# Gate and up of three feed-forwards as seven products of quarter size in a transformer trunk on one core

## The chip, the cores and the metric

The kernel runs on one core of one Trainium2 chip, as one launch. The metric is the device time of that launch in microseconds (us), the median of three runs. The times of single instructions come from one profiled execution. The engines are named as the profile names them: PE is TensorE (matmuls) and PEld its weight loads, DVE is VectorE, ACT is ScalarE, POOL is GpSimd, SP is SyncE, which here only issues DMAs.

## What is computed

A decoder trunk of two layers over 512 tokens of width 1024, in float32. Each layer is a feed-forward, a mixer and a second feed-forward, all added to the residual `h`:

```
h = h + 0.5 * swiglu(rmsnorm(h, ffn1_norm[l]), ffn1_w_gate_up[l], ffn1_w_down[l])
u = rmsnorm(h, mix_norm[l])            # layer 0: gated DeltaNet, layer 1: forgetting attention
h = h + concatenate([main, mem_out]) @ w_out[l]
h = h + 0.5 * swiglu(rmsnorm(h, ffn2_norm[l]), ffn2_w_gate_up[l], ffn2_w_down[l])

def swiglu(x, w_gate_up, w_down):      # w_gate_up: 1024 x 5632, w_down: 2816 x 1024
    gate, up = jnp.split(x @ w_gate_up, 2, axis=-1)
    return (jax.nn.silu(gate) * up) @ w_down
```

After layer 0 one projection of the normed residual gives the keys, values and gates that layer 1 attends to. The trunk ends with an rmsnorm.

## The kernel before

**Layout.** `h` lies transposed in SBUF, as 8 tiles of 128 columns of the model by 512 tokens. A float32 product is made of three passes in the fp32r type: each operand is split into a rounded part and a rest (`x_hi`, `x_lo`; `w_hi`, `w_lo`), and hi*hi, hi*lo and lo*hi are summed in PSUM (`split_products`, lines 628 to 632).

**Phases.** In order: up0, down0, gdnin0 (projections and DeltaNet), wout0, up1, down1, kv0, up2, down2, foxin0 (projections and attention), wout1, up3, down3, final. `up` is the gate and up half of a feed-forward, `down` its second half. The change touches up1, up2 and up3, the phases ahead of them (wout0, kv0, wout1) and behind them (down1 to down3). up0 stays.

**A unit of an up phase.** An up phase is 22 units. A unit makes 128 columns of gate and the same 128 columns of up for 512 tokens: 8 slices of the model's 1024 columns, times 2 outputs, times 3 passes, which is 48 matmuls of 128x512 (`unit`, line 648). Two units alternate in everything: in `raw`, `w_hi` and `w_lo` (slot u % 2) and in two pairs of PSUM banks. For each unit
- SP loads 1 MB of weights to `raw` in two DMAs as soon as the rest of the unit two before is cut (`load_gate_up`, line 486, waits for `lo_ready`),
- ACT rounds them to `w_hi` (`round_hi`, line 1359) and DVE subtracts to `w_lo` (`cut_lo`, line 1887),
- after the unit's last matmul (`unit_done`) DVE moves gate and up from PSUM to `gate_up` times `rstd`, the rmsnorm's factor per token (`scaled`, line 1910), ACT takes the silu (line 1521), POOL multiplies (line 2657), ACT rounds the product to `hid_hi` (line 1525) and DVE cuts `hid_lo` (line 2066).

Each engine runs its own instructions in the order written. They meet through semaphores only.

**Around an up phase.** The last matmuls of wout or kv complete `h` two tiles at a time. DVE adds them to `h` (line 2457), ACT rounds the tile times its gain to `x_hi` (`feed_hi`) and DVE cuts `x_lo` (`feed_lo`). ACT squares each tile and POOL adds the squares up (`add_square`, line 2624). In wout phases PE sums them over partitions behind the first up unit (`spread_sum`), ACT takes the root, and DVE the reciprocal, `rstd` (line 1907). A tile of a down phase is 22 slices of `hid` by 3 passes, 66 matmuls. Before the first of them PE waits for half of `hid` at a time.

Of the kernel before, what the change touches and what calls it, by code (L numbers as in the profile page):

```python
# [118 lines left out]
def build_trunk(nc, mem, x, ffn1_norm, ffn1_gu, ffn1_down, mix_norm, ffn2_norm, ffn2_gu, ffn2_down,  # L119
# [22 lines left out]
    with ExitStack() as ctx:  # L142
# [73 lines left out]
        x_diag = place("x_diag", [P, SEQ], at=pair_at + 6144)  # L216
        late = HEAD_UNITS * SEQ * 4
# [27 lines left out]
        mpt_at = mixer.next  # L245
# [81 lines left out]
        y_rms = y_cols.put("y_rms", [P, TT])  # L327

# [38 lines left out]
        def over_heads(a, n=HEADS):  # L367
# [28 lines left out]
        hid_hi_ready, hid_ready = sem("hid_hi_ready"), sem("hid_ready")  # L396

# [50 lines left out]
        kv_spilled, c_spilled = [sem(f"kv_spilled{b}") for b in range(2)], sem("c_spilled")  # L448
        v_back, k_back, c_back = sem("v_back"), sem("k_back"), sem("c_back")
# [169 lines left out]
        def _(pe):  # L619
# [120 lines left out]
            for name in phases:  # L740
# [87 lines left out]
                elif kind == "up":  # L828
                    unit(u, g, x_hi, x_lo, feed=KT * feeds_before[fed_by[name]])
                    if fed_by[name] != "kv0":  # L830
                        spread_sum(fed_by[name])
                    unit(u + 1, g + 1, x_hi, x_lo)
                    with pe.Fori(0, NP // 2 - 1) as i:
                        for j in range(2):
                            unit(u + 2 + j, g + 2 + j, x_hi, x_lo, i)
                elif name == LAST_DOWN:
                    free = bank_of(g)

                    def turn_residual(c):

                        if c >= TT:
                            pe.wait_ge(y_moved, c - TT + 1)
                        for t in range(TT):
                            last = nc.tensor.transpose(ps[:, TT + c % TT, t * P:(t + 1) * P],
                                                       h[:, c, t * P:(t + 1) * P], ident[:])
                        last.then_inc(y_turned, 1)

                    for x in range(2):
                        for n, tiles in enumerate(LAST_TILES):
# [24 lines left out]
                            last.then_inc(unit_done, 1)  # L874
                            if x == 0 and 1 <= n <= KT // 2:
# [8 lines left out]
                elif kind == "gdnin":  # L884
# [13 lines left out]
                    def gram_product():  # L898
# [9 lines left out]
                        last.then_inc(gram, 1)  # L908
# [1880 lines left out]
```

## Time and profile before

| | us |
|---|---|
| median of 3 runs | 1965.64 |
| lowest and highest run | 1965.41, 1966.4 |
| span of the profiled execution | 1963.3 |
| up1, up2, up3 in that span | 240.3, 239.4, 240.3 |
| busy: PE, PEld, DVE, ACT, POOL | 1955.6, 1609.9, 895.2, 742.0, 379.3 |

The span is the time from the first to the last instruction of the profiled execution, and the result behind it differs from it by the launch (2.3 us here). A busy PE says only that matmuls were in flight: they overlap, each being recorded with its latency, so PE's pace is read from the distance between their starts. A group of instructions has the mean time of one. "Idle before" names what an engine waited for. The up phases are 720 us of the span.

### The profile page before, as it was taken

Reading aid. Unit: us, or ns where it says so; the run is one execution under the profiler, and the core shown is the slowest. Engines: PE = TensorE matmul, PEld = TensorE weight load, DVE = VectorE, ACT = ScalarE, POOL = GpSimd, SP = SyncE. Lnnn points to the kernel's source line nnn. Section 1 sums busy time; section 2 is a strip of 40 time slices with the busy share of each in tenths; the row PEclk is TensorE's granted clock in tenths of the full one; section 3 lists DMA queues with packets and bytes.
Section 4 is the critical chain, followed back from the end, with each engine's and each line's share of the span. In section 5 each row is a group of like instructions: output and inputs, shape, how many; then the busy total and the mean of one; then the engine's idle time right before and its main releaser. Section 6 shows DMA issues by size and latency. Waiting matters only on the chain.

```text
span 1963.3 us, 24695 instructions
## 1 busy us (share of the span) xinstructions
PE 1955.6 (100%) x9733; PEld 1609.9 (82%) x9733; DVE 895.2 (46%) x891; ACT 742.0 (38%) x908; POOL 379.3 (19%) x265
## 2 busy tenths in 40 slices
PE   9999999999999999999999999999999999999998
PEld 8888888888877888888888888888887788888887
DVE  6544334378866533433334433433346553333223
ACT  5422222245545444432222443432235453434213
POOL 1312221112813321211010121211011032121100
PEclk9999999999999999999999999999999999999999
DMA  6343323344221333332334433333351133332321
GB/s 195 95 122 105 107 74 88 106 138 131 87 56 44 103 94 103 91 94 87 90 98 153 126 90 103 92 87 89 101 198 44 43 107 103 90 104 78 118 97 65
DMA packets 313971, 196.16 MB, mean 100 GB/s; under 512 B 18543, under 2 KB 304896, under 8 KB 313394
## 3 DMA queue, kind: packets, MB, share of 16 engines
q1 hardware_dynamic: 309872, 182.29, 32.2%
q10 hardware_dynamic: 3138, 9.79, 1.5%
q0 software_dynamic: 896, 3.16, 0.4%
q8 instruction: 47, 0.77, 0.2%
q14 instruction: 18, 0.15, 0.0%
HBM read 188.75 MB, written 6.46 MB: 99 GB/s over the span
## 4 chain that ended last, share of the span: by engine, by line
PE 97%; DVE 2%; ACT 1%; issue 0%; DMA 0%; DVEq 0%; ACTq 0%
PE ps L630 30%; PE ps L632 30%; PE ps L631 30%; PE ps L1301 1%; PE ps L1275 1%; PE ps L713 0%; PE ps L1286 0%; PE ps L735 0%; PE ps L725 0%; PE ps L1128 0%; PE ps L1006 0%; PE ps L1122 0%; PE ps L985 0%; PE ps L1102 0%; PE ps L936 0%
## 5 line engine op out<-in xcount | busy, mean ns | idle before, releaser
L630 PE MATMUL ps<-x_hi,w_hi 128*128 128x512 f32 x1790 | 706.5, 395 | 0.3
L632 PE MATMUL ps<-x_hi,w_lo 128*128 128x512 f32 x1790 | 697.1, 389 | 0.0
L631 PE MATMUL ps<-x_lo,w_hi 128*128 128x512 f32 x1790 | 696.9, 389 | 0.0
L1366 ACT ACTIVATE w_hi<-raw 128x2048 fp32r<-128x2048 f32 (+2 forms) x180 | 315.8, 1754 | 726.7 <-PE ps L632 726.7
L1892 DVE TENSOR_TENSOR w_lo<-raw,w_hi 128x2048 fp32r<-128x2048 f32 (+1 forms) x179 | 394.7, 2205 | 244.1 <-ACT w_hi L1366 244.1
L630 PEld LDWEIGHTS ps<-x_hi,w_hi 128*128 128x128 f32 x1790 | 336.2, 188 | 75.1 <-issue 4.1
L632 PEld LDWEIGHTS ps<-x_hi,w_lo 128*128 128x128 f32 x1790 | 336.0, 188 | 70.3
L631 PEld LDWEIGHTS ps<-x_lo,w_hi 128*128 128x128 f32 x1790 | 336.3, 188 | 68.1 <-issue 1.0
L1914 DVE TENSOR_TENSOR gate_up<-ps,rstd 128x1024 f32<-128x1024 f32 x88 | 107.8, 1225 | 326.7 <-PE ps L632 326.2
L2657 POOL TENSOR_TENSOR gate_up<-gate_up 128x512 f32<-128x512 f32 x66 | 145.8, 2210 | 565.8 <-ACT gate_up L1521 565.8
L630 PE MATMUL ps<-hid_hi,w_hi 128*128 128x512 f32 x528 | 205.4, 389 | 0.0
L631 PE MATMUL ps<-hid_lo,w_hi 128*128 128x512 f32 x528 | 205.4, 389 | 0.0
L632 PE MATMUL ps<-hid_hi,w_lo 128*128 128x512 f32 x528 | 205.4, 389 | 0.0
L2624 POOL TENSOR_TENSOR square_sum<-square_sum,gate_up 128x512 f32<-128x512 f32 x40 | 69.3, 1732 | 412.5 <-ACT gate_up L1381 350.3
L630 PEld LDWEIGHTS ps<-hid_hi,w_hi 128*128 128x128 f32 x528 | 99.1, 188 | 20.7
L631 PEld LDWEIGHTS ps<-hid_lo,w_hi 128*128 128x128 f32 x528 | 99.1, 188 | 20.6
L632 PEld LDWEIGHTS ps<-hid_hi,w_lo 128*128 128x128 f32 x528 | 99.1, 188 | 20.4
L2066 DVE TENSOR_TENSOR hid_lo<-gate_up,hid_hi 128x512 f32 (+1 forms) x66 | 45.7, 693 | 136.0 <-ACT hid_hi L1525 136.0
L1525 ACT ACTIVATE hid_hi<-gate_up 128x512 f32 (+1 forms) x66 | 41.9, 634 | 159.2 <-POOL gate_up L2657 159.2
L630 PE MATMUL ps<-w_hi,hid_hi 128*128 128x512 f32 x176 | 68.8, 391 | 0.0
L632 PE MATMUL ps<-w_hi,hid_lo 128*128 128x512 f32 x176 | 68.5, 389 | 0.0
L631 PE MATMUL ps<-w_lo,hid_hi 128*128 128x512 f32 x176 | 68.5, 389 | 0.0
(334 smaller groups left out, 1645.3 us busy)
## 6 DMA issues: line engine op xcount, KB each, us to landing
raw<-in_ffn_w_gate_up SPq DMA_DIRECT2D x174, 512.0 KB, 5.0
raw<-in_ffn_w_down SPq DMA_DIRECT2D x48, 384.0 KB, 3.7
raw<-in_ffn_w_down SPq DMA_DIRECT2D x48, 320.0 KB, 3.1
raw<-in_gdn_w_in SPq DMA_DIRECT2D x26, 512.0 KB, 4.8
raw<-in_ffn_w_down SPq DMA_DIRECT2D x20, 512.0 KB, 4.3
raw<-in_w_out SPq DMA_DIRECT2D x16, 512.0 KB, 4.4
raw<-in_kv_w SPq DMA_DIRECT2D x12, 512.0 KB, 4.8
raw<-in_mem_w_kv SPq DMA_DIRECT2D x8, 512.0 KB, 4.2
```

What stands on the lines that cost most here:

```text
L630: nc.tensor.matmul(dst, hi, xh, start=first, stop=False)
L631: nc.tensor.matmul(dst, hi, xl, start=False, stop=False)
L632: return nc.tensor.matmul(dst, lo, xh, start=False, stop=last)
L1275: nc.tensor.matmul(ps[:, 4 + n % 2, 0:(i + 1) * P], fq[:, hd, i * P:(i + 1) * P], fk[:, hd, 0:(i + 1) * P], start=True, stop=True).then_in ...
L1301: last = nc.tensor.matmul(ps[:, b1 + hd % 2, i * P:(i + 1) * P], fv[:, s, hd * P:(hd + 1) * P], fpt[m % 2][:, s * P:(s + 1) * P], start=s ...
L1366: nc.scalar.activation(w_hi[s][:, 0:n], raw[s][:, 0:n], ACT.Copy).then_inc(hi_ready, 1)
L1525: nc.scalar.activation(hid_hi[:, bass.ds(at, 1), :], gate_up[:, j, 0:1, :], ACT.Copy).then_inc(hid_hi_ready, 1)
L1892: nc.vector.tensor_tensor(w_lo[s][:, 0:n], raw[s][:, 0:n], w_hi[s][:, 0:n].bitcast(F32), ALU.subtract).then_inc(lo_ready, 1)
L1914: nc.vector.tensor_tensor(dst, src, by, ALU.mult).then_inc(evac, 1)
L2066: nc.vector.tensor_tensor(hid_lo[:, bass.ds(at, 1), :], gate_up[:, j, 0:1, :], hid_hi[:, bass.ds(at, 1), :].bitcast(F32), ALU.subtract).th ...
L2624: nc.gpsimd.tensor_tensor(square_sum[:, 0:tokens], square_sum[:, 0:tokens], gate_up[:, b, 0, 0:tokens], ALU.add).then_inc(sum_ready, 1)
L2657: nc.gpsimd.tensor_tensor(gate_up[:, j, 0, :], gate_up[:, j, 0, :], gate_up[:, j, 1, :], ALU.mult).then_inc(prod_ready, 1)
```

## The change

**The scheme.** In up1 to up3 the product of a unit is seen as a 2x2 block product: the model's tiles are taken as even and odd ones (4 pairs), the outputs as gate and up, the tokens as two halves of 256. Seven products of blocks replace the eight: each is 4 pairs by 3 passes, 12 matmuls of 128x256, so 84 in a unit. Three products take a weight block as loaded (`direct`, 1536 words of a row), four take a sum of blocks (`sums`, four blocks of 512 words, S1 to S4). Four take plain quarters of `x` or its difference T1, and three the differences T4, T2, T3 of `x` (`t_x`).

**Sums of weights.** POOL makes S1 and S3 (`first_sum`, `third_sum`), DVE S2 and S4 (`second_sum`). ACT rounds and DVE cuts the direct blocks (1536 words), S1 with S2, and S4 with S3 (1024 each). Direct parts now always lie in the one slot of `w_hi` and `w_lo`, sums in the other, so each is rewritten while its own unit runs, once the products that read it are done.

**Results.** DVE puts gate and up together from seven parts in PSUM with four additions and scales gate alone; ACT first copies the first product's part (`first_taken`). POOL writes the product of silu(gate) and up to a new `hid`. Up is no longer scaled: the down phases scale by `rstd` instead (one more DVE instruction for each of 8 tiles in down1 and down2; `y_half` in down3). The split of `hid` into `hid_hi` and `hid_lo` moves behind the units: 22 tiles in a row from the last unit on, since its place holds `t_x` and `sums` until then, and down waits for them tile by tile.

**Feeding.** wout0, kv0 and wout1 also make the differences of `x` (`even_source`, `pair_columns`) and the first unit's sums (`seven_lead`, `seven_lead_more`, `seven_lead_last`). Many semaphores are shared under new names with the same meaning (`left`).

```diff
+            def seven_unit(name, u, g, n, i=0, spread=False):
...
+                pe.wait_ge(direct_lo, NP * x + n + 1 + 2 * i)
+                bank_free(g + n, i)
+                seven_product(to[1], direct_at(u, 0), operands("B11")).then_inc(product_done, 1)
+                seven_product(to[4], direct_at(u, 1), operands("T4"))
+                seven_product(to[2], direct_at(u, 2), operands("B21")).then_inc(product_done, 1)
+                pe.wait_ge(sums_lo, (NP + 1) * x + n + 2 + 2 * i)
+                seven_product(to[5], sum_at(u, S1), operands("T1")).then_inc(product_done, 1)
+                seven_product(to[6], sum_at(u, S2), operands("T2")).then_inc(product_done, 1)
+                pe.wait_ge(lo_ready, u + n + 1 + 2 * i)
+                pe.wait_ge(part_taken, NP * x + n + 1 + 2 * i)
+                seven_product(to[3], sum_at(u, S4), operands("B22")).then_inc(product_done, 1)
+                if spread:
+                    pe.wait_ge(rms_ready, sums_before[fed_by[name]] + 1)
+                seven_product(to[7], sum_at(u, S3), operands("T3")).then_inc(unit_done, 1)
...
-                    if hid_wait is not None:
-                        pe.wait_ge(hid_ready, hid_wait + (half + 1) * HALF)
+                        if hid_wait is not None:
+                            pe.wait_ge(hid_ready, hid_wait + n + 1)
...
+                    def step(n, j, i=0, more=True, root=False):
...
+                            last_sums(n, i)
+                            if root:
+                                root_mean_square(fed_by[name], rstd[:], bank=bank_of(g + 1) + 5)
+                            silu(n - 1, 1 - j, i)
+                        take_first(n, j, i)
+                        if more:
+                            act.wait_ge(product_done, at + 2 + 2 * DONE * i)
...
+                            nc.scalar.activation(direct(w_hi, slot(u)), direct_blocks(slot(u + n + 1))[:, :, 1:4, :],
+                                                 ACT.Copy).then_inc(direct_hi, 1)
...
+                        if more:
+                            first_sums(n + 1, at + 4, i)
...
+                        even_source(name, n)
+                        odd_hi(name, n)
...
+                        if n == 2:
+                            seven_lead(feeds[name], u + 4)
+                        even_hi(name, n)
+                        t_hi(name, n)
...
+                    def partial_sums(n, j, i=0):
...
+                        nc.vector.tensor_tensor(two_halves(up), over_heads(first_taken[:, j, :], 2),
+                                                two_halves(ps[:, b + 1, :]), ALU.add).then_inc(gate_step, 1)
+                        dve.wait_ge(gate_step, 4 * (NP * x + n) + 1 + 8 * i)
+                        nc.vector.tensor_tensor(two_halves(gate), over_heads(up[:, TOK:], 2),
+                                                two_halves(ps[:, b + 4, :]), ALU.add).then_inc(gate_step, 1)
...
                     def step(n, j, i=0):
...
+                        if n:
+                            gates(n - 1, 1 - j, i)
+                            if n == 1 and normed:
+                                last_sums(n)
+                                reciprocal_of_rms(fed_by[name], rstd[:])
+                            gate_scale(n - 1, 1 - j, i)
+                            if n > 1 or not normed:
+                                last_sums(n, i)
+                        second_sum(name, u, n + 1, i)
+                        direct_cut(name, u, n + 1, i)
...
+                        partial_sums(n, j, i)
+                        first_sums(n + 1, i)
+                        up_second(n, j, i)
...
+                        first_sum(u, n + 1, sums_used + n + 2, i)
+                        if n:
+                            product(n - 1, 1 - j, i)
+                        third_sum(u, n + 1, i)
```

**The order on DVE in the loop over units.** One unit of up1's loop before; the names are the kernel's tiles.

```order
L1914 TENSOR_TENSOR gate_up<-ps,rstd 128x1024 [waits unit_done]
L1891 REGISTER_ALU
L1892 TENSOR_TENSOR w_lo_64<-raw_62,w_hi_63 128x2048 [waits hi_ready]
L2064 REGISTER_ALU
L2066 ISA [waits hid_hi_ready]
L2066 TENSOR_TENSOR hid_lo<-gate_up,hid_hi 128x512
```

The same engine and loop after the change, without its register rows:

```order
L2498 TENSOR_TENSOR gate_up<-gate_up,ps 128x512 [waits gate_step]
...
L2504 TENSOR_TENSOR gate_up<-gate_up,rstd 128x512 [waits evac]
...
L2304 TENSOR_TENSOR w_lo_67<-sums,w_hi_66 128x1024 [waits hi_ready]
...
L2289 TENSOR_TENSOR sums<-sums,raw_62 128x512 [waits pool_sum]
L2292 TENSOR_TENSOR sums<-raw_62,sums 128x512 [waits dve_sum]
L2298 TENSOR_TENSOR w_lo_64<-raw_62,w_hi_63 128x1536 [waits direct_hi]
...
L2480 TENSOR_TENSOR gate_up<-first_taken,ps 128x512 [waits prod_ready]
...
L2483 TENSOR_TENSOR gate_up<-gate_up,ps 128x512 [waits gate_step]
...
L2304 TENSOR_TENSOR w_lo_67<-sums,w_hi_66 128x1024 [waits sums_hi]
...
L2490 TENSOR_TENSOR gate_up<-gate_up,ps 128x256 [waits gate_step]
```

Three instructions of a unit became ten; four of the ten read PSUM, six read SBUF alone.

**The order on POOL in the same loop.** Before, one unit:

```order
L2657 TENSOR_TENSOR gate_up<-gate_up 128x512 [waits silu_ready]
```

After, one unit:

```order
L3168 TENSOR_TENSOR sums<-raw_62 128x512 [waits sums_lo]
L3207 REGISTER_ALU
L3208 ISA [waits silu_ready]
L3208 TENSOR_TENSOR hid<-gate_up 128x512
L3175 REGISTER_ALU
L3176 TENSOR_TENSOR sums<-raw_62 128x512 [waits lo_ready]
```

The product now stands between two sums of weights.

**The order on DVE from the last wout0 tiles into up1.** After the change only, from the sums of unit 0 on; before, the same stretch is one addition to `h`, two cuts of `x_lo`, one of weights and the reciprocal.

```order
L2289 TENSOR_TENSOR sums<-sums,raw_62 128x512 [waits pool_sum]
L2292 TENSOR_TENSOR sums<-raw_62,sums 128x512 [waits dve_sum]
L2298 TENSOR_TENSOR w_lo_64<-raw_62,w_hi_63 128x1536 [waits direct_hi]
L2304 TENSOR_TENSOR w_lo_64<-sums,w_hi_63 128x512 [waits sums_hi]
L2304 TENSOR_TENSOR w_lo_67<-sums,w_hi_66 128x1024 [waits sums_hi]
...
L2270 TENSOR_TENSOR t_x<-t_f,t_x 128x3x256 [waits t_hi_ready]
L2304 TENSOR_TENSOR w_lo_67<-sums,w_hi_66 128x512 [waits hi_ready]
L2289 TENSOR_TENSOR sums<-sums,raw_65 128x512 [waits pool_sum]
L2292 TENSOR_TENSOR sums<-raw_65,sums 128x512 [waits dve_sum]
L2298 TENSOR_TENSOR w_lo_64<-raw_65,w_hi_63 128x1536 [waits direct_hi]
```

All of it is queued ahead of what PE waits for: L2298 first for unit 0, last for unit 1.

## Rows read from the trace of the kernel before

**Rows 1.** The page: busy time of the engines, and what the chain of waits lies on.

```profile
PE 1955.6 (100%) x9733; PEld 1609.9 (82%) x9733; DVE 895.2 (46%) x891; ACT 742.0 (38%) x908; POOL 379.3 (19%) x265
...
PE 97%; DVE 2%; ACT 1%; issue 0%; DMA 0%; DVEq 0%; ACTq 0%
```

**Rows 2.** Windows over up1 and up2: length, PE, PEld, DVE, ACT, POOL, clock, DMA.

```profile
663.20:903.50 240.30, 240.30 (x1059) 198.65 (x1059) 95.94 (x68) 95.66 (x89) 50.86 (x23) 1.00 0.34 93
1095.00:1334.40 239.40, 239.40 (x1058) 198.23 (x1057) 92.17 (x67) 93.32 (x85) 46.08 (x22) 1.00 0.34 95
```

**Rows 3.** Timeline of PE (start, length): matmuls of 512 columns, then of 256.

```profile
88.20 0.39 PE L631 MATMUL ps<-x_lo,w_hi 128*128 128x512 f32 x1
...
90.46 0.39 PE L632 MATMUL ps<-x_hi,w_lo 128*128 128x512 f32 x1
...
91.04 0.28 PE L630 MATMUL ps<-xm_hi,w_hi 128*128 128x256 f32 x1
...
95.84 0.28 PE L631 MATMUL ps<-xm_lo,w_hi 128*128 128x256 f32 x1
```

**Rows 4.** Timeline of DVE in up1 (start, length, idle before).

```profile
707.86 1.23 DVE L1914 TENSOR_TENSOR gate_up<-ps,rstd 128x1024 f32<-128x1024 f32 x1 [3.87 <-PE ps L632]
709.82 2.29 DVE L1892 TENSOR_TENSOR w_lo<-raw,w_hi 128x2048 fp32r<-128x2048 f32 x1 [0.73 <-ACT w_hi L1366]
```

**Rows 5.** Groups of DVE and ACT by form (count, busy, mean ns, idle before).

```profile
L2214 DVE TENSOR_TENSOR low<-low,decay 128x1536 f32<-128x1536 f32 x1 | 1.8, 1759 | 0.2 <-ACT decay L1699 0.2
L1892 DVE TENSOR_TENSOR w_lo<-raw,w_hi 128x1024 fp32r<-128x1024 f32 x4 | 4.9, 1225 | 17.5 <-ACT w_hi L1366 17.5
L2232 DVE TENSOR_TENSOR z<-ps,rstd 128x512 f32<-128x512 f32 x6 | 4.1, 686 | 1.7 <-PE ps L632 1.6
L2364 DVE TENSOR_TENSOR v_new<-v_tok,ps 128x256 f32<-128x256 f32 x7 | 2.9, 421 | 3.5 <-PE ps L1102 3.5
L1907 DVE RECIPROCAL rstd<-rstd 128x512 f32<-128x512 f32 x5 | 16.8, 3354 | 19.5 <-ACT rstd L1385 19.5
L1366 ACT ACTIVATE w_hi<-raw 128x1024 fp32r<-128x1024 f32 x4 | 4.2, 1060 | 23.9 <-PE ps L632 23.9
L1699 ACT ACTIVATE decay<-decay 128x1536 f32<-128x1536 f32 x1 | 1.5, 1492 | 1.4 <-DVE decay L2204 1.4
L1525 ACT ACTIVATE hid_hi<-gate_up 128x512 f32 x60 | 38.1, 634 | 145.0 <-POOL gate_up L2657 145.0
```

**Rows 6.** Timeline of POOL in up1.

```profile
875.01 1.45 POOL L2657 TENSOR_TENSOR gate_up<-gate_up 128x512 f32<-128x512 f32 x1 [9.43 <-ACT gate_up L1521]
884.46 2.88 POOL L2657 TENSOR_TENSOR gate_up<-gate_up 128x512 f32<-128x512 f32 x1 [8.00 <-ACT gate_up L1521]
```

**Rows 7.** Timeline of DVE beside the second of them, and beside POOL in down0.

```profile
883.89 2.29 DVE L1892 TENSOR_TENSOR w_lo<-raw,w_hi 128x2048 fp32r<-128x2048 f32 x1 [0.73 <-ACT w_hi L1366]
...
295.26 0.75 DVE L1898 SCALAR_TENSOR_TENSOR x_lo<-h,gains,x_hi  x1 [1.37 <-ACT x_hi L1369]
295.93 2.72 DVE L1892 TENSOR_TENSOR w_lo<-raw,w_hi 128x1408 fp32r<-128x1408 f32 x1
...
295.75 1.41 POOL L2624 TENSOR_TENSOR square_sum<-square_sum,gate_up 128x512 f32<-128x512 f32 x1 [12.92 <-ACT gate_up L1381]
```

**Rows 8.** Timeline of DVE and POOL in the DeltaNet: a DVE read of PSUM first.

```profile
575.45 1.23 DVE L2223 COPY k<-ps 128x1024 f32<-128x1024 f32 x1 [2.52 <-PE ps L1006]
...
576.79 1.69 DVE L1936 TENSOR_TENSOR mp<-mp,m_stat 128x1024 f32<-128x1024 f32 x1
...
575.50 1.90 POOL L2723 TENSOR_TENSOR k_tok<-k_tok,gate_exp 128x1024 f32<-128x1024 f32 x1 [38.07 <-PE ps L1006]
```

**Rows 9.** Groups of POOL by form, flat rows and short ones.

```profile
L2647 POOL TENSOR_TENSOR mem_sum<-mem_sum,mem_sq 128x256 f32<-128x256 f32 x7 | 5.2, 736 | 8.7 <-ACT mem_sq L1499 8.3
L2702 POOL TENSOR_TENSOR tri<-tri,tri_tmp 96x256 f32<-96x256 f32 x1 | 1.1, 1061 | 0.1
```

**Rows 10.** The page's DMA issues: the weights of gate and up, with the time to landing.

```profile
raw<-in_ffn_w_gate_up SPq DMA_DIRECT2D x174, 512.0 KB, 5.0
```

More of the change, by code:

```diff
@@ L75 @@
 MEM_SCORES_BESIDE = 12
+SEVEN = ("up1", "up2", "up3")
+TOK = SEQ // 2
+PAIRS = KT // 2
+BLOCK_W = PAIRS * P
+DIRECT_W = 3 * BLOCK_W
+T4, T2, T3 = 0, 1, 2
+S1, S2, S4, S3 = 0, 1, 2, 3
+DONE = 5
+T4_TILES, T2_TILES, T3_TILES, SUM_TILES, TAKEN_TILES = 2, 6, 10, 14, 18
 def fox_block(n):
@@ L216, in build_trunk @@
         x_diag = place("x_diag", [P, SEQ], at=pair_at + 6144)
+        TILE_B = SEQ * 4
+        t_x = place("t_x", [P, 3, 2, PAIRS, TOK], F32R, at=lo_at + T4_TILES * TILE_B)
+        t_f = place("t_f", [P, 3, 2, PAIRS, TOK], at=lo_at + T4_TILES * TILE_B)
+        sums = place("sums", [P, 4, BLOCK_W], at=lo_at + SUM_TILES * TILE_B)
+        taken = Region(lo_at + TAKEN_TILES * TILE_B, (NP - TAKEN_TILES) * TILE_B)
+        first_taken = taken.put("first_taken", [P, 2, TOK])
+        even_f = {name: place(f"even_f_{name}", [P, PAIRS, SEQ], at=h_at + at)
+                  for name, at in (("wout0", 12 << 10), ("kv0", 12 << 10), ("wout1", 40 << 10))}
         late = HEAD_UNITS * SEQ * 4
@@ new lines, in seven_part, with direct_at, sum_at @@
+            def seven_part(dst, weights, x_of, kk, first=False, last=False):
+                w_s, at = weights(kk)
+                xh, xl = x_of(kk)
+                return split_products(dst, w_hi[w_s][:, at:at + P], w_lo[w_s][:, at:at + P], xh, xl,
+                                      first and kk == 0, last and kk == PAIRS - 1)
+            def direct_at(u, q):
+                return lambda kk: (slot(u), (3 * kk + q) * P)
+            def sum_at(u, r):
+                return lambda kk: (slot(u + 1), r * BLOCK_W + kk * P)
@@ new lines, in seven_regions, with seven_product @@
+            def seven_regions(g0):
+                b = bank_of(g0)
+                lo_cols, hi_cols = slice(0, TOK), slice(TOK, SEQ)
+                return {1: ps[:, b, lo_cols], 3: ps[:, b, hi_cols],
+                        2: ps[:, b + 1, lo_cols], 6: ps[:, b + 1, hi_cols],
+                        4: ps[:, b + 4, lo_cols], 5: ps[:, b + 4, hi_cols], 7: ps[:, b + 5, lo_cols]}
+            def seven_product(dst, weights, x_of):
+                for kk in range(PAIRS):
+                    last = seven_part(dst, weights, x_of, kk, first=True, last=True)
+                return last
@@ new lines, in _ @@
+                    step(0, 0)
+                    step(1, 1, root=fed_by[name] != "kv0")
+                    with act.Fori(0, NP // 2 - 2) as i:
+                        for j in range(2):
+                            step(2 + j, j, i)
+                    step(NP - 2, 0)
+                    step(NP - 1, 1, more=False)
+                    for tile in range(4, T3_TILES):
+                        split_hi(tile)
+                    silu(NP - 1, 1)
+                    round_hi(u + NP + 1)
+                    for tile in range(T3_TILES, NP):
+                        split_hi(tile)
@@ L1828, in _ @@
-                            act.wait_ge(f_a, 2)
-                            nc.scalar.activation(t, t, ACT.Ln, bias=ones[0:HEADS, 0:1]).then_inc(f_a, 1)
-                        if n == HEADS - 1:
-                            for c in range(KT - 1):
-                                act.wait_ge(x_free, N_REL * releases[name] + c + 1)
-                                feed_hi(x_hi[:, c, :], h[:, c, :], gains[:, gain + c:gain + c + 1])
+                            act.wait_ge(row_d, left["row_d"] + 1)
@@ L2075, in _ @@
+                    split_lo(3)
+                    partial_sums(NP - 1, 1)
+                    up_second(NP - 1, 1)
+                    split_lo(4)
+                    gates(NP - 1, 1)
+                    gate_scale(NP - 1, 1)
+                    for tile in range(5, T3_TILES):
+                        split_lo(tile)
+                    cut_lo(u + NP + 1)
+                    for tile in range(T3_TILES, NP):
+                        split_lo(tile)
                 elif name == LAST_DOWN:
```

632 lines of the change are left out of this document (493 added, 139 removed).

## The prediction

> **What bounds the kernel now.** Read first the page's engine line and its chain of waits [rows 1]: PE is busy all through, and the chain lies on it for 97%. Then the windows over up1 and up2 [rows 2]: PE fills both at a granted clock of 1.00 (2.4 GHz), while DVE is busy for 96 and 92 of 240 us, ACT for 96 and 93, POOL for 51 and 46. Up3 reads like up1. The profiled execution (1963.3 us, and 2.3 outside) equals the median to 0.1 us, so its rows can be added to 1965.6. 239.4 us for 22 units is 10.88 us a unit, and up1's and up3's further 0.5 us is `spread_sum`. The weights' loads take 5.0 us to land, half a unit [rows 10]: SP isn't the question. So a shorter product counts in full, until another engine needs more than PE. A busy share of 40% leaves room, but the change fills just that.
>
> **PE, removed and added.** Ten starts of 512-column matmuls take 2.26 us and forty of 256 columns 4.80 us [rows 3]: 226 and 120 ns each; by the length of the phase, 239.4 / (22 x 48), the first is 226.7, which I take. A unit goes from 48 x 0.2268 = 10.89 us (the phase gives the same) to 84 x 0.120 = 10.08. Seven eighths would be 9.53: half the width costs more than half the time. The gain is 0.81 us a unit, 53 us over 66 units, if PE stays the bound. The Trainium skill, "TensorE: Matmul & The Clock Gate", section Back-to-back issue gap, gives columns / 2.4 GHz + 2.5 ns for a lone matmul; by that, an estimate, a unit goes from 10.36 to 9.17 and gains 1.19. The rows contradict it in both widths (226.8 and 120 ns against 215.8 and 109.2), and I go by the rows.
>
> **DVE, a steady unit.** Before: 1.23 to empty PSUM, 2.29 for the cut [rows 4], 0.69 for `hid_lo`, 4.2 us. After: six operations of 512 (gate's second part, its scale, S2, S4, two partial sums) at 0.69, two cuts of 1024 at 1.22, one of 1536 at 1.76, one addition of 256 at 0.42 [rows 5]. That is 4.14 + 2.44 + 1.76 + 0.42 = 8.76. An instruction in a row starts 0.08 us before the one ahead is through (295.93 behind 295.26 + 0.75 [rows 7]), one that needs the other's result just behind it; with five or so such overlaps I take 8.40. Alone it would fit under 10.08, with 1.7 us to spare.
>
> **DVE against POOL.** POOL used to have one operation of 512 a unit, now three. Alone that takes 1.45 us, beside a cut 2.88 [rows 6]: it started 0.57 us into the cut and ended 1.16 us after its end at 886.18 [rows 6, 7]. Nor is DVE spared: a cut of 1408 took 2.72 us behind a POOL addition that had begun 0.18 us before [rows 7], where 1.22 for 1024 and 1.76 for 1536 [rows 5] put it at some 1.62; and `mp` took 1.69 instead of 1.23 until POOL's multiplication was through [rows 8]. Reading PSUM, a DVE copy kept its 1.23 beside POOL [rows 8]. So operations of SBUF inputs alone exclude each other between DVE and POOL, first come first served, and PSUM reads are free. Of POOL's 1.45 us the first 0.3 need no lock and some 1.15 do: that is what it worked on after the cut's end. The Trainium skill, "SBUF — State Buffer", section Who interferes with whom, says the same and against this change: the port pair that the two share is an exclusive lock held for the whole instruction, taken by a DVE instruction with two SBUF inputs. By the page all 1.45 would count, 4.35 for three; the rows show 1.15 each.
>
> Now lay the two orders beside each other. `first_sum` is released by the first sums' cut and runs beside `up_second` and the gate's addition, both PSUM reads: only its last 0.31 us holds up the scale. `product` is released by the silu (512 words, about the 0.63 of `hid_hi` [rows 5]) and two handoffs of under 0.1, some 0.75 us behind the scale, while DVE is in the last sums' cut (1.22), so it is next in line and has the lock just ahead of S2: 1.09. `third_sum` is released by that same cut and starts behind `product`, while S2 runs; it gets the lock ahead of S4: 0.98. Sum 2.38, and DVE's unit is 8.40 + 2.38 = **10.78 us, 0.70 over PE's 10.08**. DVE becomes the bound: the direct cut of the next unit, last in this row, is what PE waits for (`direct_lo`). Of 0.81 us a unit 0.11 is left. POOL (3 x 1.45, with its waits 5.3) and ACT (1.06 + 0.63 for the silu + at most 0.63 for the copy + 1.49 + 1.06 = 4.9 us [rows 5]) have room; what ACT costs hangs on its place in the chain.
>
> **Start of up1 and up3.** Here DVE has the new feeding (four differences and three cuts where two cuts stood), and POOL its additions of squares. Laid out from the end of the last but two weights of wout, with the same durations: the last wout unit waits 0.84 us for its weights' cut, which stands behind the second pair's feeding; unit 0 of up waits 2.15 for the direct cut, behind S2 and S4, each held up 1 us by an addition of squares; inside unit 0, the last pair's `x` and T parts come 2.85 late. Unit 1 waits 3.8 for its direct cut: `first_sum` stands behind the last addition of squares (1.45), then come first_sum 1.45, S2 0.69 + 1.13, S4 0.69 and the cut 1.76. In unit 1 PE's P3 waits 2.6 for `first_taken`: ACT's copy stands behind the silu, that behind the scale, that behind the reciprocal of 3.35 us [rows 5]. Unit 2 waits another 0.3. Sum 12.6, less two shorter units (1.6): **+11.0 us**. Before, the reciprocal was hidden: nobody but the evacuation two units on waited for it.
>
> **The phases.** Up1: +11.0; 19 units at 10.78 for 10.89, -2.0; the last at PE's pace, -0.8; and down1. Its first tile, 66 x 0.2268 = 15.0 us on PE, now waits tile by tile for 22 cuts of 0.69 (15.2) on DVE, which start about 3 us after the units' end (scale 0.69, silu 0.62, product 1.45 and one rounding 0.63); 18.6 in all, +3.6. Together +11.8. Up3: the same start; down3 uses each tile of `hid` for four times as many matmuls (2.7 us), which hides the cuts: +8.2. Up2 is fed from kv0, with the squares and the reciprocal done: PE's pace for the first four units and the last (-4.0), 17 at 10.78 (-1.9), the same 0.8 ahead of its first unit, and +3.6 in down2: -1.5. The scale in down1 and down2 lies beside 15 us of PE, except behind the last tile: +0.5 with what hangs on it. Sum 11.8 + 8.2 - 1.5 + 0.5 = +19.0: **1985 us**. Within this case the handoffs may be 0.05 us longer each (10.89 a unit, +8 over three phases) or the start's waits 2 to 5 us shorter each: 1973 to 1997.
>
> **Rivals.**
> *PE stays the bound (faster, the other side).* Place: the turn of DVE's loop where `product` and `third_sum` stand. Price: what is blocked must stay under 10.08 - 8.40 = 1.68 us a unit; 2.38 is my sum. It does if one of the two falls beside the partial sums, which read PSUM, for instance because the scale comes later and `product` meets `second_sum` when that is already under way; then one block of 1 us goes. POOL's own delay is harmless. Then up1 gives -1.6 (start +11.0, 20 units x -0.81, down +3.6), up3 -5.2 (no down), up2 -14.2 (22 units, down2), the scales +0.5: 1945. If in addition the starts overlap better (unit 1 needs no more than 1 us), 1933. For it: POOL has 4.8 us of slack, and which of two comes first hangs on 0.1 us. Against it: in the steady order both sums' places are fixed by the same cut.
> *POOL's sums are slower.* No row of before shows a POOL operation that picks blocks of a row. 736 ns for a flat 128x256 and 1061 for the same 256 cut in short pieces [rows 9] bound it at 1.45 and 2.1 for 512; the sums' pieces are whole blocks of 128 or more words, nearest to the flat form. At 1.6, a unit is 11.08 (each 0.15 counts twice) and the sum is +19 + 0.3 x 19 x 3 = +36: 2002.
> *POOL's sums cost 1.35.* 10.48 a unit: 19 x 3 x 0.3 = 17 us less: 1967, no change.
> *The clock.* Before, no window shows less than 1.00 [rows 2], since PE never paused. Now it pauses for up to 3.8 us twice. If its clock falls to 1.2 GHz there, one unit of 10 us may run at half speed: up to +10 for a start, in the upper part of my range.
> *The change does less than it says:* the matmuls' count is plain in the code; excluded.
>
> **How the numbers follow.** DVE-bound as laid out 0.44, 1985 (1973 to 1997, slower). Slower sums on POOL 0.20, 2002 (slower). Shorter ones 0.08, 1967 (same). PE-bound 0.28 (faster), of it 0.20 near 1945 and 0.08 near 1933. The range leaves out the last and the tail above 2008: 1940 to 2008. A measurement here tells 0.2%, 4 us, from no change, so faster than 1961.7 is 0.28, between 0.08, above 1969.6 is 0.64.
>
> **What the profile after would show.** PE's 256-column starts 120 ns apart (else the gain is wrong). DVE busy for about 10.7 of each 10.8 us in up1's middle, PE's idle before P1 put down to `w_lo` of the direct cut; with PE bound, DVE idle before its gate addition instead. S2 and S4 at 1.7 us each where I take them blocked, at 0.69 where not. POOL's sums at 1.45. PE's third and second waits of 2 to 4 us in the first two units of up1 and up3, none such in up2. Tiles of `hid` in down1 0.69 us apart. The prediction is wrong if S2 and S4 are short: then the whole steady term turns to -0.8 a unit.

## The result, and the profile after

The changed kernel takes 1988.8 us (median of four runs, 1988.13 to 1990.04) against 1965.53 for the kernel before: a ratio of 1.012, 95% interval 1.0105 to 1.0134. It is slower by 23 us, the forecast was slower by 19 (1985.0).

The profile's page of the changed kernel: busy time of the engines, and the chain of waits. Before [rows 1], DVE was busy for 895 us and the chain lay on PE for 97%.

```profile
PE 1930.9 (97%) x12113; PEld 1688.2 (85%) x12113; DVE 1387.8 (70%) x1499; ACT 802.2 (40%) x1076; POOL 524.5 (26%) x397
...
PE 73%; DVE 14%; issue 6%; POOL 3%; ACT 2%; DMA 1%; DVEq 0%; SPq 0%; ACTq 0%; POOLq 0%
```

Two windows of the same kernel (length, PE, PEld, DVE, ACT, POOL, granted clock, DMA share, GB/s), one over 17 units in the middle of up1 and one over the first half of its unit 1:

```profile
700.00:880.00 180.00, 175.37 (x1429) 172.01 (x1428) 177.66 (x171) 74.76 (x85) 75.40 (x52) 1.00 0.36 99
683.00:690.00 7.00, 6.50 (x42) 6.50 (x43) 6.86 (x8) 1.99 (x3) 1.28 (x1) 0.76 0.03 9
```

DVE is busy for 177.7 of 180 us where it was busy for 96 of 240 [rows 2]. What PE waited for, over the whole span (total, times, longest); the kernel before shows none of these lines in its up and down phases:

```profile
PE ps L680 <- DVE w_lo L2298: 25.4, 63, 2.8
PE ps L680 <- DVE w_lo L2208: 11.4, 4, 5.8
PE ps L680 <- DVE hid_lo L2520: 5.2, 6, 1.0
PE ps L680 <- DVE t_x L2270: 2.9, 2, 1.6
PE ps L680 <- ACT first_taken L1746: 2.1, 2, 1.0
```

L2298 is the direct cut, 63 waits in 66 units. Its row in the steady part, and three matmul rows that give the pitch of 256 columns (compare rows 3): 0.12 us from start to start, ten steps in 1.20.

```profile
707.24 0.38 PE L680 MATMUL ps<-x_hi,w_hi 128*128 128x256 f32 x1 [0.28 <-DVE w_lo L2298]
...
714.53 0.28 PE L680 MATMUL ps<-x_hi,w_hi 128*128 128x256 f32 x1
...
715.73 0.28 PE L681 MATMUL ps<-x_lo,w_hi 128*128 128x256 f32 x1
```

A wait of 0.28 us in its latency's shadow costs a unit 0.5 us. The units of up1 start 17.0, 13.1, then 10.60 us apart (19 times, the last of them 10.66), and the last one takes 10.17. The stretches of the two executions, each from the start of its first matmul to that of the next stretch's (the first begins a quarter into the last wout0 unit but one):

| stretch (us) | before | after | difference | forecast |
|---|---|---|---|---|
| wout0's last two units and up1 | 259.4 | 264.5 | +5.1 | +8.2 |
| down1 | 119.7 | 123.3 | +3.6 | +3.6 |
| kv0 and up2 | 311.2 | 306.2 | -5.0 | -5.1 |
| down2 | 119.7 | 123.3 | +3.6 | +3.6 |
| foxin0, wout1, up3 | 380.2 | 389.9 | +9.7 | +8.2 |
| down3 and the end | 129.1 | 135.4 | +6.3 | 0 |

With -0.3 ahead of wout0 this is the 23.1 us between the two spans. The forecast's 0.5 us for the scales of down1 and down2 together is in no row.

One unit of DVE's row in up1 (start, length; idle before is shown where there is any), and POOL's of the same unit; the rows of before are rows 4, 6 and 7.

```profile
800.76 1.75 DVE L2298 TENSOR_TENSOR w_lo<-raw,w_hi 128x1536 fp32r<-128x1536 f32 x1
802.43 0.68 DVE L2480 TENSOR_TENSOR gate_up<-first_taken,ps 128x512 f32<-128x512 f32 x1
803.14 0.69 DVE L2483 TENSOR_TENSOR gate_up<-gate_up,ps 128x512 f32<-128x512 f32 x1
803.75 1.22 DVE L2304 TENSOR_TENSOR w_lo<-sums,w_hi 128x1024 fp32r<-128x1024 f32 x1
804.88 0.41 DVE L2490 TENSOR_TENSOR gate_up<-gate_up,ps 128x256 f32<-128x256 f32 x1
805.33 0.69 DVE L2498 TENSOR_TENSOR gate_up<-gate_up,ps 128x512 f32<-128x512 f32 x1
806.05 0.84 DVE L2504 TENSOR_TENSOR gate_up<-gate_up,rstd 128x512 f32<-128x512 f32 x1
806.81 1.21 DVE L2304 TENSOR_TENSOR w_lo<-sums,w_hi 128x1024 fp32r<-128x1024 f32 x1
807.94 1.78 DVE L2289 TENSOR_TENSOR sums<-sums,raw 128x512 f32<-128x512 f32 x1
809.76 1.67 DVE L2292 TENSOR_TENSOR sums<-raw,sums 128x512 f32<-128x512 f32 x1
811.36 1.75 DVE L2298 TENSOR_TENSOR w_lo<-raw,w_hi 128x1536 fp32r<-128x1536 f32 x1
...
805.04 1.30 POOL L3168 TENSOR_TENSOR sums<-raw 128x512 f32<-128x512 f32 x1 [4.75 <-DVE w_lo L2304]
807.74 1.44 POOL L3208 TENSOR_TENSOR hid<-gate_up 128x512 f32 x1 [1.40 <-ACT gate_up L1752]
809.14 1.75 POOL L3176 TENSOR_TENSOR sums<-raw 128x512 f32<-128x512 f32 x1
```

The reader sees ten DVE operations from 800.76 to 811.36 with nothing between them, and among six of 512 words two that take 1.78 and 1.67 us instead of 0.69. S2 (L2289) is through 0.54 us after POOL's product ends at 809.18; S4 (L2292) 0.54 us after POOL's third sum ends at 810.89. The third sum itself takes 1.75 instead of 1.30 since it waits for S2. The scale (L2504) loses 0.15 to the first sum, and the two additions beside that sum, which read PSUM, nothing.

### The profile page after: what moved, and what is told of

It reads as the page before. It is cut to its first block, busy times and chain, and to the rows that moved or that the text cites. A ratio compares the mean times of both kernels' runs of the same rounds, so it can differ in the third digit from the quotient of the medians.

```text
span 1986.4 us, 31460 instructions
## 1 busy us (share of the span) xinstructions
PE 1930.9 (97%) x12113; PEld 1688.2 (85%) x12113; DVE 1387.8 (70%) x1499; ACT 802.2 (40%) x1076; POOL 524.5 (26%) x397
## 4 chain that ended last, share of the span: by engine, by line
PE 73%; DVE 14%; issue 6%; POOL 3%; ACT 2%; DMA 1%; DVEq 0%; SPq 0%; ACTq 0%; POOLq 0%
PE ps L680 23%; PE ps L682 22%; PE ps L681 22%; DVE w_lo L2298 6%; POOL tri L3265 2%; POOL tri_tmp L3263 1%; DVE hid_lo L2520 1%; DVE w_lo L2208 1%; DVE sums L2289 1%; PE ps L1442 1%; PE ps L1468 1%; DVE rstd L2223 1%; DVE w_lo L2304 0%; ACT w_hi L1533 0%; PE ps L1453 0%
## 5 line engine op out<-in xcount | busy, mean ns | idle before, releaser
L680 PE MATMUL ps<-x_hi,w_hi 128*128 128x256 f32 (+1 forms) x1790 | 601.7, 336 | 29.0 <-DVE w_lo L2298 25.4
L682 PE MATMUL ps<-x_hi,w_lo 128*128 128x256 f32 (+1 forms) x1790 | 586.4, 328 | 0.0
L681 PE MATMUL ps<-x_lo,w_hi 128*128 128x256 f32 (+1 forms) x1790 | 586.0, 327 | 0.0
L2208 DVE TENSOR_TENSOR w_lo<-raw,w_hi 128x2048 fp32r<-128x2048 f32 (+2 forms) x113 | 245.4, 2172 | 176.2 <-ACT w_hi L1533 176.2
L680 PE MATMUL ps<-t_x,w_hi 128*128 128x256 f32 x792 | 225.0, 284 | 2.9 <-DVE t_x L2270 2.9
L681 PE MATMUL ps<-t_x,w_hi 128*128 128x256 f32 x792 | 224.8, 284 | 0.0
L682 PE MATMUL ps<-t_x,w_lo 128*128 128x256 f32 x792 | 224.5, 283 | 0.0
L1601 ACT ACTIVATE w_hi<-sums 128x1024 fp32r<-128x1024 f32 (+1 forms) x135 | 140.2, 1040 | 182.2 <-PE ps L682 159.7
L2304 DVE TENSOR_TENSOR w_lo<-sums,w_hi 128x1024 fp32r<-128x1024 f32 (+1 forms) x135 | 161.2, 1195 | 0.0
L680 PEld LDWEIGHTS ps<-t_x,w_hi 128*128 128x128 f32 x792 | 153.0, 193 | 3.3 <-DVE t_x L2270 3.3
L681 PEld LDWEIGHTS ps<-t_x,w_hi 128*128 128x128 f32 x792 | 152.7, 193 | 0.0
L682 PEld LDWEIGHTS ps<-t_x,w_lo 128*128 128x128 f32 x792 | 152.7, 193 | 0.0
```

The source lines that it names most:

```text
L680: nc.tensor.matmul(dst, hi, xh, start=first, stop=False)
L681: nc.tensor.matmul(dst, hi, xl, start=False, stop=False)
L682: return nc.tensor.matmul(dst, lo, xh, start=False, stop=last)
L1601: nc.scalar.activation(w_hi[s][:, at:at + (r1 - r0) * BLOCK_W], sums[:, r0:r1, :].rearrange("p r n -> p (r n)"), ACT.Copy).then_inc(signal, 1)
L2208: nc.vector.tensor_tensor(w_lo[s][:, 0:n], raw[s][:, 0:n], w_hi[s][:, 0:n].bitcast(F32), ALU.subtract).then_inc(lo_ready, 1)
L2304: nc.vector.tensor_tensor(w_lo[s][:, cols], sums[:, r0:r1, :].rearrange("p r n -> p (r n)"), w_hi[s][:, cols].bitcast(F32), ALU.subtract). ...
```

## Experiments

Every experiment is an edit of the changed kernel. Times stand against its 1988.8 us, and the kernel before ran at 1965.2 to 1965.5 beside each of them.

### x1: POOL's third sum behind the direct cut

```
 def third_sum(u, n, i=0, cuts=None):
     if n:
         pool.wait_ge(lo_ready, u + n + 2 * i)
+    if cuts is not None:
+        pool.wait_ge(direct_lo, cuts + 2 * i)
...
-    third_sum(u, n + 1, i)
+    third_sum(u, n + 1, i, NP * seven_index(name) + n + 2)
```

> The changed kernel with one more wait: POOL's third_sum starts only when DVE's direct cut of the same unit is through, so that it falls beside DVE's two partial sums, which read PSUM, instead of beside S4. Theory (DVE is the bound because POOL's operations lock it out): S4 falls from 1.58 to 0.69 us, a unit from 10.60 to PE's 10.08, 57 units x -0.52 = -30 us, 1959 us (1955 to 1963). Rival 1 (what is blocked only moves, onto the first sums' cut behind the partial sums): S4 short, but that cut 0.5 to 1 us longer, a unit of 10.4 to 10.6, 1977 to 1989. Rival 2 (a unit's length hangs on DVE's own work and the handoffs, not on POOL): no change.

Measured: 1952.12 us (1951.06 to 1952.68), ratio to before 0.9931 (0.9914 to 0.9948). The units are 10.08 us apart. The same part of a unit, DVE then POOL, in up1:

```profile
802.77 0.69 DVE L2292 TENSOR_TENSOR sums<-raw,sums 128x512 f32<-128x512 f32 x1
803.76 1.76 DVE L2298 TENSOR_TENSOR w_lo<-raw,w_hi 128x1536 fp32r<-128x1536 f32 x1 [0.30 <-ACT w_hi L1796]
805.44 0.68 DVE L2480 TENSOR_TENSOR gate_up<-first_taken,ps 128x512 f32<-128x512 f32 x1
806.15 0.69 DVE L2483 TENSOR_TENSOR gate_up<-gate_up,ps 128x512 f32<-128x512 f32 x1
806.76 1.29 DVE L2304 TENSOR_TENSOR w_lo<-sums,w_hi 128x1024 fp32r<-128x1024 f32 x1
...
805.67 1.30 POOL L3178 TENSOR_TENSOR sums<-raw 128x512 f32<-128x512 f32 x1 [3.47 <-DVE w_lo L2298]
```

The same sum, begun 0.23 us into the first partial sum, costs DVE 0.07 us (on the cut at 806.76) instead of 1: two operations that read PSUM cover it. S2's block by the product stays (S2 takes 1.70 us in the mean). DVE now waits for ACT (0.30), and a unit is PE's 84 x 0.12 again. One more wait on POOL gives 36.7 us, more than the 30 expected: in the profiled executions the three up phases are 32.4 us shorter, and down1, down2 and down3 1.5, 1.5 and 1.8, since the cuts of `hid` start earlier. Rival 1 and 2 are out. This version beats the kernel before by 13 us.

### x2: POOL's sums made short

```
-    nc.gpsimd.tensor_tensor(by_pair(sums[:, S1, :]), blocks[:, :, 0, :], blocks[:, :, 2, :],
+    nc.gpsimd.tensor_tensor(by_pair(sums[:, S1, :])[:, :, 0:w], blocks[:, :, 0, 0:w], blocks[:, :, 2, 0:w],
...
-    nc.gpsimd.tensor_tensor(by_pair(sums[:, S3, :]), blocks[:, :, 1, :], blocks[:, :, 0, :],
+    nc.gpsimd.tensor_tensor(by_pair(sums[:, S3, :])[:, :, 0:w], blocks[:, :, 1, 0:w], blocks[:, :, 0, 0:w],
```

(w is 128 in unit 0 of a phase and 4 in the others.)

> The changed kernel with POOL's two sums of weights cut to 4 x 4 words of a row in all units behind the first of a phase, so most of S1 and S3 keeps old values; every semaphore and all of DVE's, ACT's and PE's work stay. Theory (lock): without two of POOL's three operations a unit of up takes PE's 10.08 us; S4 0.69 and S2 0.69 to 1.75, as product still meets it or not; with the starts 1950 to 1957 us in all. Rival (DVE's own chain or ACT's order sets 10.60): units stay at 10.5 to 10.6, 1980 to 1988.

Measured: 1948.3 us in a single run, units 10.08 us apart, S4 0.72 us in the mean of 66 and S2 still 1.70:

```profile
L2289 DVE TENSOR_TENSOR sums<-sums,raw 128x512 f32<-128x512 f32 x66 | 112.1, 1699 | 8.3 <-POOL sums L3170 8.3
L2292 DVE TENSOR_TENSOR sums<-raw,sums 128x512 f32<-128x512 f32 x66 | 47.7, 722 | 2.3
```

The kernel leaves most of S1 and S3 unwritten, so it shows the time alone. S4 lost what the third sum took, S2 kept what the product takes. With DVE's own work untouched the unit fell to PE's 10.08, so 10.60 was POOL's doing.

### x4: unit 1's first sum ahead of the last two squares

```
 for c in range(KT):            # POOL, wout
     add_square(name, c % 2, c)
...
+    if c == 5:
+        first_sum(u + KT // 2, 1, (NP + 1) * seven_index(feeds[name]) + 2)
```

> The changed kernel with the first sum of unit 1 of up1 and up3 moved on POOL ahead of the last two additions of squares of wout. Theory (unit 1 waits 3.6 us for its direct cut since first_sum stands behind those additions, and the pause lowers PE's clock for some 1.5 us more): the wait falls to under 1 us, the slow matmuls behind it go, 2 x (3 + 1.4) = -9 us, 1980 us. Rival (DVE's work is what unit 1 waits for; the additions, now beside S2 and S4, lock it out for as long): the wait falls by 1 to 2 us, 1984 to 1987.

Measured: 1985.39 us, 3.4 less. The waits of PE in the last wout0 unit and the first two units of up1, the changed kernel and then this one:

```profile
PE ps L680 <- DVE w_lo L2298: 4.8, 2, 2.8
PE ps L680 <- ACT first_taken L1746: 1.0, 1, 1.0
```

```profile
PE ps L680 <- DVE w_lo L2298: 2.9, 2, 1.9
PE ps L680 <- ACT first_taken L1746: 2.5, 1, 2.5
```

The wait ahead of unit 1 falls from 2.83 us (not the expectation's 3.6) to 0.98, and the one for `first_taken` in unit 1 grows from 1.05 to 2.53: four fifths of the 1.85 us are given back at the next wait. DVE's own rows say why, S2 of unit 1 in the changed kernel, then S2, S4 and the direct cut in this one:

```profile
679.30 1.75 DVE L2289 TENSOR_TENSOR sums<-sums,raw 128x512 f32<-128x512 f32 x1 [3.87 <-POOL sums L3168]
```

```profile
675.87 1.79 DVE L2289 TENSOR_TENSOR sums<-sums,raw 128x512 f32<-128x512 f32 x1
677.69 1.68 DVE L2292 TENSOR_TENSOR sums<-raw,sums 128x512 f32<-128x512 f32 x1
679.29 2.84 DVE L2298 TENSOR_TENSOR w_lo<-raw,w_hi 128x1536 fp32r<-128x1536 f32 x1
```

The 3.87 us in which DVE stood idle for POOL's sum are gone, but now S4 and the direct cut, 0.69 and 1.75 us in the changed kernel, stand beside squares and the third sum and take 2.1 us more. That is the rival. My theory that POOL's queue alone held unit 1 falls.

### x5: ACT's copy ahead of silu in unit 1

```
         silu(n - 1, 1 - j, i)   # now only for n > 1
     take_first(n, j, i)
+    if n == 1:
+        silu(0, 0)
```

> The changed kernel with ACT's copy of unit 1's first product put ahead of silu of unit 0, which stands behind the scale and that behind the reciprocal. Theory (PE's wait of 1.05 us for first_taken in up1 and 1.02 in up3 is that order): both waits go, -2.4 us with what follows each, 1986.4 us. Rival (DVE has the rest of that stretch full, so that unit 2 waits for its direct cut instead): unit 2 starts when it did, 1988 to 1989.

Measured: 1988.77 us (1987.43 to 1990.24), no change. The wait for `first_taken` is gone, and the direct cut has a third one in the same stretch:

```profile
PE ps L680 <- DVE w_lo L2301: 6.2, 3, 2.8
```

It was 4.8 in two, and is 6.2 in three. Unit 1 and unit 2 start when they did (17.0 and 13.15 us apart). The rival holds: the direct cut of unit 2 starts on DVE at 694.57 instead of 694.74, and PE meets it there.

### x8: squares made short

```
-    add_square(name, c % 2, c)
+    add_square(name, c % 2, c, tokens=SEQ if c < 4 else 8)
```

> The changed kernel with POOL's additions of squares of tiles 4 to 7 in wout0 and wout1 cut to 8 of 512 tokens, so the norm ahead of up1 and up3 is that of half the model for most tokens. Theory (POOL's squares lock DVE out in the feeding, and hold up first_sum of unit 1): S2 and S4 of unit 0 0.69 instead of 1.78 and 1.70 us, unit 0 starts 2 us earlier, and unit 1's wait of 3.6 us falls to 1 or less; with the clock's share 4 to 6 us for each of up1 and up3, 1977 to 1981 us. Rival (the new feeding itself, seven DVE operations for each pair, sets the start): under 2 us for each, 1985 to 1988.

Measured: 1981.7 us in a single run, 7 less. Unit 0 of up1 takes 14.9 instead of 17.0 us and unit 0 of up3 13.5; the wait ahead of unit 1 is under 0.7 us; and again there is one of 2.15 us for `first_taken` (1.05 before). Counted over the stretches of the table, up1 is done 3.7 us sooner and up3 3.1. So POOL's squares and their place account for 3 to 4 us of each start, less than I expected. The rest I put down to the new feeding on DVE; no run took that away.

### x6 and x9: down weights earlier, in all three phases and in the last alone

```
+    round_hi(u + NP + 1)      # ACT, ahead of the last silu
     silu(NP - 1, 1)
-    round_hi(u + NP + 1)
...
-    for tile in range(5, T3_TILES):    # DVE
-        split_lo(tile)
+    split_lo(5)
     cut_lo(u + NP + 1)
+    for tile in range(6, T3_TILES):
+        split_lo(tile)
```

> The changed kernel with the second block of down weights rounded ahead of the last silu (ACT) and cut ahead of all but one of the tiles of hid that stood before it (DVE), in all three up phases. Theory (in down3 PE waits 3.7 us for this cut and then runs slow for 2 us): -5.5 us, 1983 us, down1 and down2 as before. Rival (the tiles of hid, now later, are waited for in its place): the wait in down3 becomes one for hid_lo of 1 to 2 us, and down1 and down2 are 1 to 2 us longer each, 1986 to 1990.

> The edit of x6 in up3 alone. In x6 down3 fell from 129.3 to 125.3 us while down1 and down2 grew by 2.9 and 1.8, where PE now waited for tiles of hid. Theory (it helps only where a tile of hid lasts PE 2.7 us): -4 us, 1984.8. Rival (down3's gain belongs to a shift that the other two made): no change.

Measured: 1989.53 (1987.14 to 1989.57) with all three, 1984.48 (1984.24 to 1984.58) with the last alone. In the first, down3 is 4.0 us shorter, but down1 2.9 and down2 1.8 longer: there a tile of `hid` lasts PE 0.68 us, and PE waits for the tiles that the cut pushed back. The waits in down1 of the first kernel, and the one left in down3 of the second (3.65 us in the changed kernel):

```profile
PE ps L680 <- DVE hid_lo L2520: 3.2, 2, 2.2
```

```profile
PE ps L680 <- DVE w_lo L2211: 0.9, 1, 0.9
```

So the cut that is early in one phase is late in the other, and the edit pays where a tile of `hid` is used for 12 matmuls.

### x11: the weights of wout's last unit cut earlier

```
+    if n == 1:
+        cut_lo(u + 3)
     feed_pair(name, n)
-    if n == 1:
-        cut_lo(u + 3)
```

(ACT's rounding of the same weights likewise ahead of its part of the feeding.)

> The changed kernel with the weights of wout's last unit rounded and cut ahead of the feeding of the second pair of tiles, in wout0 and wout1. In wout1 PE waits 5.84 us for that cut, which the prediction had at 0.8. Theory (DVE has feeding, cuts and sums without a gap from there to unit 0's direct cut, so this pause of PE is not on the path): the pause shrinks to under 1 us and unit 0 of up3 starts when it did, within 1 us of 1609; 1987 to 1990. Rival (the wait costs what it shows): unit 0 of up3 starts 4 to 6 us earlier, 1983 to 1985.

Measured: 1988.06 us (1987.74 to 1988.37), within 1 us of the changed kernel. PE's waits from 1575 to 1640 us, the changed kernel and this one:

```profile
PE ps L680 <- DVE w_lo L2208: 5.8, 1, 5.8
PE ps L680 <- DVE w_lo L2298: 3.5, 2, 2.8
```

```profile
PE ps L680 <- DVE w_lo L2298: 10.3, 2, 7.4
```

The pause of 5.8 us is gone, and a pause of 7.4 stands ahead of unit 0 of up3, which starts at 1608.05 instead of 1609.22. Half a microsecond of that was gained before down2; from the start of foxin0 to the end of up3 the kernels differ by 0.7 us. That is what the longest wait in the profile cost.

### x7 and x10: together

> Four edits together: third_sum behind the direct cut (as in x1), first_sum of unit 1 ahead of the last two squares (as in x4), in unit 1 of each phase ACT's copy of the first product ahead of silu, and the second block of down weights earlier in up3 alone. Theory (each takes away a wait of its own): from 1952.1 a unit 1 shorter by 2.5 us and by what the slow clock behind a pause costs, 1.4, in up1 and up3 (-8), -4 in down3: 1940 us (1937 to 1944). Rival (the starts hang on DVE's sum of work, and what is saved at one wait is met at the next): only down3's 4 us and 1 to 2 in each start, 1945 to 1948.

Measured: 1945.22 us (1941.92 to 1946.88), ratio to before 0.9901 (0.9884 to 0.9917). That is in the rival's range: against x1 down3 gave 3.8 us, up1 2.1 and up3 2.8 (229.0 us each). Unit 2 now waits for its direct cut, 1.5 us in up1 and up3, behind the reciprocal (the next expectation says 1.66 and 1.69).

> x7 with one more edit: in step 1 of each phase DVE makes unit 2's S2, S4 and direct cut ahead of the reciprocal and the scale of unit 0, and ACT takes silu of unit 0 last in that step. Theory (in x7 unit 2 waits 1.66 and 1.69 us for its direct cut, which stands behind the reciprocal's 3.35 us): that wait goes and nothing follows, -3.3 us from x7, 1942 us (1938 to 1944). Rival (the reciprocal now holds up the partial sums and the cut of unit 2's first sums, which P5 of unit 2 waits for): the wait turns up at P5, 1944 to 1947.

```
     gates(n - 1, 1 - j, i)
-    if n == 1 and normed: last_sums(n); reciprocal_of_rms(...)
-    gate_scale(n - 1, 1 - j, i)
+    if n == 1: last_sums(n)
     second_sum(name, u, n + 1, i)
     direct_cut(name, u, n + 1, i)
+    if n == 1: reciprocal_of_rms(...); gate_scale(0, 0)
```

Measured: 1944.13 us (1943.14 to 1944.77), ratio to before 0.9893 (0.9876 to 0.9909): 1 us from the former, inside the spread of both. The 1.5 us wait went and three came in unit 2 and 3 of up1, for the cuts of sums (0.40 and 0.88) and the direct cut (1.03). The rival again. It has the lowest median of all versions, 21 us ahead of the kernel before; against x7 nothing is shown, whose runs go down to 1941.92.

## Why the prediction came out right

**The pitch of the matmuls** (120 ns, 10.08 us a unit) was as read: the products take 84 x 0.12. By the formula of the Trainium skill for a lone matmul ("TensorE: Matmul & The Clock Gate", section Back-to-back issue gap) a unit would take 9.17 us, an estimate. It does not hold here: x1's units, with PE as the bound, take 10.08.

**DVE as the bound through the lock** was right in kind and nearly in size. Forecast blocks 0.31, 1.09 and 0.98 us; shown 0.15 for the scale, 1.09 for S2 and 0.98 for S4 in the unit above (in the mean of 66 units 0.13, 1.06 and 0.89). The unit came out at 10.60, not 10.78: the term that was mis-sized is the block of the scale, 0.16 of the 0.18 us, because POOL's first sum takes 1.30 us and not the 1.45 of its product, which I took for it; in 57 units the 0.18 is 10 us. The third sum is as short when nothing holds it up (1.30 in x1), yet S4's block came out at the 0.98 forecast with 1.45. So "each 0.15 counts twice" was not borne out, and the rival with sums of 1.35 was wrong in its own sum too: by that rule its unit is 10.58 and not 10.48.

The Trainium skill, "SBUF — State Buffer", section Who interferes with whom, calls the port pair of DVE and GpSimd an exclusive lock, which a DVE instruction with two SBUF inputs needs as well. The rows agree: S2 began 0.20 us behind POOL's product and ended 0.54 behind its end, and the third sum, begun while S2 ran, took 1.75 us instead of 1.30.

**The starts.** In up1 unit 0 began 2.1 us late (2.15 forecast), took 17.0 (17.2, with `spread_sum`) and unit 1 13.1 (13.0): unit 2 started 33.7 us after wout's due end, 33.2 forecast. That agreement is luck in part. The wait for the last T part was 1.28 us where I had 2.85 for the late parts, the one ahead of unit 1 2.83, not 3.8, and the one for `first_taken` 1.05, not 2.6. The clock, which I had as a bound only, made up for them: matmuls at half pace lost PE 1.5 us in unit 0 and 1.6 in unit 1.

In wout1 the start cost 5 us more than in wout0. I had taken both as alike. In wout1 the first two pairs of tiles come complete 2.6 us apart (8.0 in wout0), so two times 8 us of addition, cuts and feeding stand in a row on DVE ahead of the cut of the last unit's weights, and PE waits 5.84 us for it where I had 0.84. The step that failed is "Up3: the same start".

What ends such a phase is not the sum of PE's waits in it. It is DVE, at the place where its row without gaps begins, the direct cut of unit 2:

| us, up1 | that cut starts | up1 ends | between |
|---|---|---|---|
| changed kernel | 694.74 | 908.27 | 213.53 |
| x4 | 693.44 | 906.89 | 213.45 |
| x5 | 694.57 | 908.36 | 213.79 |
| x8 | 691.57 | 905.07 | 213.50 |
| x11 | 693.69 | 907.21 | 213.52 |

So PE's waits could be moved without much gain, by x4, x5 and x11. Ahead of that cut DVE does have gaps, 3.87 us for POOL's first sum and 1.02 for ACT's rounding in up1, and 0.6 to 0.9 for ACT at several places of the feedings; the 3.87 were the largest, and x8 brought the cut forward by 3.2 us.

**Up2** gave -5.0 for -5.1, by chance: no four units at PE's pace, but 11.3, 10.7 and then 10.60 at once (some 3 us more), against some 3 us less in the steady ones.

**Down1 and down2**: +3.6 each, as forecast, in three waits of up to 1 us. The first tile takes 18.58 us (18.6 forecast) for 14.96; behind it nothing is lost, and the 0.5 us for the scales did not come.

**Down3** was wrong, +6.3 where nothing was forecast. "down3 uses each tile of `hid` for four times as many matmuls (2.7 us), which hides the cuts" is true of the tiles of `hid`, but the second block of weights stands in the same DVE queue behind five of them, and ACT's rounding of it behind the last silu: 3.65 us of wait, and 1.6 more of slow clock behind it. I costed the cuts that the change moved and not what it moved them in front of. x9 removes 4.0 of it.

These misses (-10 in the steady units, +3 in up2's first ones, +5 in up3's start, +6 in down3) nearly cancel, by luck; 1988.8 for 1985 says less than the table by stretches does.

## What to carry to other kernels

Where POOL and DVE work in turn on SBUF alone, put POOL's operations beside those of DVE that read PSUM: one wait more on POOL was worth 37 us here, and turned a change that loses 1.2% into one that gains 0.7%. When an engine goes from 40% to 98% busy, the waits that the profile shows behind it are places where it is met, not causes: removing one moves it (5.8 us removed, 7.4 in its place). Look for the gaps in the row of that engine instead, ahead of the place from which it has none. When a step is moved to another place in a queue, cost also what stands behind it there.

## What the runs showed of the hardware

PE's clock fell behind pauses. The kernel before never pauses in these phases and holds 1.00 [rows 2]. The changed kernel's windows show 0.76 after the pause of 2.83 us ahead of unit 1. In down3, after 3.65 us of waiting, matmuls of 512 columns start 0.427 us apart from 1862.10 to 1865.09, where the granted clock is half of full, 1.2 GHz (the second and third row are in that stretch, the last behind it):

```profile
1860.92 0.50 PE L680 MATMUL ps<-w_hi,hid_hi 128*128 128x512 f32 x1 [3.65 <-DVE w_lo L2208]
...
1862.53 0.63 PE L682 MATMUL ps<-w_hi,hid_lo 128*128 128x512 f32 x1
1862.95 0.63 PE L680 MATMUL ps<-w_hi,hid_hi 128*128 128x512 f32 x1
...
1865.37 0.40 PE L680 MATMUL ps<-w_hi,hid_hi 128*128 128x512 f32 x1
```

Such a stretch costs PE 1.0 to 2.5 us, begins at the restart or up to 1.7 us behind it, and is of unequal length behind the same pause (1.0 us lost in the changed kernel and 2.2 in the one with ACT's copy ahead, both after 5.84 us). It does not follow every pause: in x11 PE stood for 2.90 us ahead of unit 0 of up1, and its matmuls kept 0.12 us until the next wait of over 1 us, 8.4 us on. In up1 and up3 of the changed kernel DVE has no wait for PE of over 0.1 us from the second pair of wout's tiles on, so what PE loses to the clock there does not reach the end of the phase; in down3, where PE is the bound, it does. Whether the clock makes the spread from run to run is not shown: it is 0.3 us in x9, 0.6 in x11 and 5.0 in x7, all with such pauses, and 0.6 to 1.6 in the kernel before.

In four kernels (x4, x6, x8, x9) PE's units behind a start went at 10.1 to 10.3 us for two or three and then settled at 10.60. The loop between DVE and POOL has only the one pace: in x4 its direct cuts start at 693.44, 704.04 and 714.62 in the same stretch. DVE was some 1.4 us ahead of PE there, and PE used that up at 0.5 us a unit.
